# mLSTM row values spread over the partitions by DMA through DRAM, the experts' row numbers on GpSimd, and the launch's first loads in quarters

## The reference

```python
for layer in range(DEPTH):                       # DEPTH = 2
    h = rms_norm(x, norm1_w[layer])
    x = x + hybrid_mixer(h, w_in[layer], ...)    # z = h @ w_in; retention, dilated attention, mLSTM; gates; w_out
    h = rms_norm(x, norm2_w[layer])
    if layer % 2 == 0: x = x + swiglu(h, w_gate, w_up, w_down)
    else:              x = x + moe_swiglu(h, w_router, b_router, w_gate, w_up, w_down)

# in mlstm, per chunk; b is the running sum of the log forget gates, ib the input gate
D  = where(causal, b[:, None] - b[None, :] + ib[None, :], -inf)
m  = maximum(b + mm, max(D, -1));  Dw = exp(D - m[:, None])
s  = (q @ k.T) * Dw

# in moe_swiglu
logits = ht @ w_router + b_router
top_v, top_i = top_k(logits, 2);  probs = softmax(top_v)
for e in range(8):
    a = silu(ht @ w_gate[e]) * (ht @ w_up[e])
    out += gates[:, e:e+1] * (a @ w_down[e])
```

## Time and profile before

| | us |
|---|---|
| median of 3 runs | 1759.18 (1758.77 to 1760.2) |
| the profiled execution's own time | 1759.04 |
| its span | 1757.3 |
| PE busy | 1744.9 (99%) |
| DVE busy | 1388.0 (79%) |
| ACT busy | 1101.2 (63%) |
| POOL busy | 87.6 (5%) |

### The profile page before, as it was taken

The page is one execution under the profiler, slowest core; times in us unless marked ns, Lnnn a source line. Parts: engine busy times, 40 slices in busy tenths (PEclk is TensorE's granted clock), DMA queues, the critical chain, the costliest instruction groups (busy, mean ns, idle before and its releaser), DMA issues.

```text
span 1757.3 us, 22823 instructions
## 1 busy us (share of the span) xinstructions
PE 1744.9 (99%) x8418; PEld 1453.8 (83%) x8418; DVE 1388.0 (79%) x1179; ACT 1101.2 (63%) x976; POOL 87.6 (5%) x72
## 2 busy tenths in 40 slices
PE   9999999999999999999999999999999999999998
PEld 8888888888888888897888888888888888888887
DVE  7966587555688665879888889889888888898898
ACT  4445564434443566537777777777777777777775
POOL 1020000000000300001000000000000000000100
PEclk9999999999999999989999999999999999999999
DMA  8553365554445523557999999999999999999995
GB/s 318 192 192 120 120 240 216 192 191 133 179 168 176 183 72 121 214 216 264 400 348 413 381 351 407 373 365 396 347 399 385 348 413 372 358 403 373 369 413 197
DMA packets 218986, 497.11 MB, mean 283 GB/s; under 512 B 8080, under 2 KB 12432, under 8 KB 218768
## 3 DMA queue, kind: packets, MB, share of 16 engines
q1 hardware_dynamic: 215808, 483.70, 74.5%
q0 software_dynamic: 3120, 12.60, 1.8%
HBM read 490.49 MB, written 7.87 MB: 284 GB/s over the span
## 4 chain that ended last, share of the span: by engine, by line
PE 95%; DVE 2%; ACT 1%; DMA 1%; issue 0%; SPq 0%; DVEq 0%; ACTq 0%
PE ps L663 30%; PE ps L664 29%; PE ps L665 29%; PE ps L672 4%; PE ps L668 3%; DVE sb_wlo L395 1%; DMA sb_ringa<-in_w_in_dram 1%; ACT sb_w L1332 0%; DVE sb_wlo L366 0%; ACT sb_whi L359 0%; ACT sb_ahi L1389 0%; DVE sb_z L1706 0%; ACT L1332 0%; DVE sb_wlo L1657 0%; ACT sb_z L1382 0%
## 5 line engine op out<-in xcount | busy, mean ns | idle before, releaser
L395 DVE TENSOR_TENSOR sb_wlo<-sb_z,sb_whi 128x2048 fp32r<-128x2048 f32 x334 | 756.0, 2289 | 99.6 <-ACT sb_whi L389 99.0
L389 ACT ACTIVATE sb_whi<-sb_z 128x2048 fp32r<-128x2048 f32 x333 | 634.1, 1925 | 175.4 <-PE ps L665 171.2
L663 PE MATMUL ps<-sb_whi,sb_hhi 128*128 128x512 f32 (+1 forms) x1752 | 686.8, 392 | 3.5 <-DVE sb_wlo L395 2.5
L664 PE MATMUL ps<-sb_whi,sb_hlo 128*128 128x512 f32 (+1 forms) x1752 | 677.9, 387 | 0.0
L665 PE MATMUL ps<-sb_wlo,sb_hhi 128*128 128x512 f32 (+1 forms) x1752 | 677.5, 387 | 0.0
L663 PEld LDWEIGHTS ps<-sb_whi,sb_hhi 128*128 128x128 f32 x1752 | 329.7, 188 | 72.5 <-issue 4.5
L665 PEld LDWEIGHTS ps<-sb_wlo,sb_hhi 128*128 128x128 f32 x1752 | 329.6, 188 | 68.7
L664 PEld LDWEIGHTS ps<-sb_whi,sb_hlo 128*128 128x128 f32 x1752 | 330.0, 188 | 64.2
L366 DVE TENSOR_TENSOR sb_wlo<-sb_z,sb_whi 128x2048 fp32r<-128x2048 f32 (+1 forms) x74 | 158.5, 2146 | 82.1 <-ACT sb_whi L359 81.8
L359 ACT ACTIVATE sb_whi<-sb_z 128x2048 fp32r<-128x2048 f32 (+1 forms) x75 | 135.2, 1807 | 138.3 <-PE ps L665 138.2
L663 PE MATMUL ps<-sb_whi,sb_ahi 128*128 128x512 f32 x560 | 220.1, 393 | 1.1 <-DVE sb_alo L1614 1.1
(11 more groups left out here) (270 smaller groups left out, 986.5 us busy)
## 6 DMA issues: line engine op xcount, KB each, us to landing
sb_z<-in_moe_w_gate_dram SPq DMA_DIRECT2D x112, 1024.0 KB, 7.1
sb_z<-in_moe_w_up_dram SPq DMA_DIRECT2D x112, 1024.0 KB, 7.7
sb_z<-in_moe_w_down_dram SPq DMA_DIRECT2D x112, 1024.0 KB, 6.8
sb_ringa<-in_w_in_dram SPq DMA_DIRECT2D x43, 1024.0 KB, 4.8
sb_z<-in_w_in_dram SPq DMA_DIRECT2D x24, 1024.0 KB, 5.4
sb_z<-in_ffn_w_up_dram SPq DMA_DIRECT2D x10, 1024.0 KB, 5.0
sb_z<-in_ffn_w_gate_dram SPq DMA_DIRECT2D x10, 1024.0 KB, 4.9
sb_z<-in_ffn_w_down_dram SPq DMA_DIRECT2D x10, 1024.0 KB, 4.9
```

The costliest lines, as they stand in the source:

```text
L389: nc.scalar.activation(e_lane(s)[0], ringb[:, s % RING_B, :], ACT.Copy).then_inc(hi_done, 1)
L395: nc.vector.tensor_tensor(lo, ringb[:, s % RING_B, :], hi.bitcast(F32), ALU.subtract).then_inc(split, 1)
L663: nc.tensor.matmul(out, lh, rh, start=start, stop=False)
L664: nc.tensor.matmul(out, ll, rh, start=False, stop=False)
```

## The change

Three things. The mLSTM row values go to DRAM and come back to all partitions by DMAs of Pool, and the DVE adds the mask in place. The two batches `slots()` and `slot_ids()` leave the DVE; Pool computes the same numbers with other instructions (sums over eight experts are made by halving). The launch's first loads are cut in quarters, and the squares of x stand later on the DVE. The constants' load of the launch leaves out `sel` (512 of 4352 columns).

```diff
@@ -442,11 +444,13 @@
-            sp.dma_start(x[:, :, 0:C], xin[:, :, 0:C]).then_inc(x_in, 16)
+            sp.dma_start(x[:, :, 0:C // 2], xin[:, :, 0:C // 2]).then_inc(x_in, 16)
             sp.dma_start(const[:, 0:P], a["const"][:, 0:P]).then_inc(ident_in, 16)
             sp.dma_start(small[:, :], a["small"]).then_inc(small_in, 16)
-            first = part(a["w_in"][0], 0, KH // 2, IN_QK, C)
-            sp.dma_start(raw_slot(0, "A", 0)[:, 0:SLOT // 2].rearrange("p (k n) -> p k n", n=C), first).then_inc(raw_first, 16)
+            for k, landed in enumerate((raw_first, raw_second)):
+                sp.dma_start(raw_slot(0, "A", 0)[:, k * C:(k + 1) * C],
+                             a["w_in"][0][k * P:(k + 1) * P, IN_QK:IN_QK + C]).then_inc(landed, 16)
+            sp.dma_start(x[:, :, C // 2:C], xin[:, :, C // 2:C]).then_inc(x_more, 16)
@@ -462,7 +466,7 @@
                 if layer == 0:
-                    sp.dma_start(const[:, P:], a["const"][:, P:]).then_inc(consts_in, 16)
+                    sp.dma_start(const[:, P:CONST["sel"][0]], a["const"][:, P:CONST["sel"][0]]).then_inc(consts_in, 16)
@@ -566,6 +570,17 @@
+            def spread_rows(layer):
+                pool.wait_ge(rows_ok, layer + 1)
+                pool.dma_start(ml_rows, rows[:, 1, :]).then_inc(ml_stored, 16)
+                pool.wait_ge(ml_stored, 16 * (layer + 1))
+                pool.wait_ge(rpv_mm, layer + 1)
+                every = ml_rows.rearrange("(a b) s -> a b s", a=2).unsqueeze(0).to_broadcast([P, 2, 2, S])
+                for a_ in range(2):
+                    pool.dma_start(blkm[:, a_, :, 0:S], every[:, a_]).then_inc(spread_in, 16)
+                    pool.dma_start(blkm[:, a_, :, S:BLK], every[:, a_, :, P:S]).then_inc(spread_in, 16)
@@ -599,6 +614,7 @@
                 inverse_root(rrs, rss, RDV, root_ok)
+                spread_rows(layer)
                 inverse_root(mrs, mss, MDV, root_ok)
@@ -611,6 +627,68 @@
+            links = [0]
+            def link(ins):
+                links[0] += 1
+                ins.then_inc(pool_chain, 1)
+                pool.wait_ge(pool_chain, links[0])
+            rowx, item_ = lg, rtmp
+            both = stat(268, 32).rearrange("p (c t n) -> p c t n", c=2, t=TT)
+            pos = root[:, 0:16].rearrange("p (t n) -> p t n", t=TT)
+            part = root[:, 16:48].rearrange("p (c t n) -> p c t n", c=2, t=TT)
+            late, early = root[:, 48:50], root[:, 50:52]
+            term = root[:, 52:60].rearrange("p (a c t) -> p a c t", a=2, c=2)
+            per_token = lambda v: v.unsqueeze(1).to_broadcast([P, TT, NE])
+            per_choice = lambda v: v.unsqueeze(1).to_broadcast([P, 2, TT, NE])
+            def chosen(out, src):
+                link(pool.tensor_tensor(part, both, per_choice(src), ALU.mult))
+                link(pool.tensor_tensor(part[:, :, :, 0:4], part[:, :, :, 0:4], part[:, :, :, 4:8], ALU.add))
+                link(pool.tensor_tensor(part[:, :, :, 0:2], part[:, :, :, 0:2], part[:, :, :, 2:4], ALU.add))
+                link(pool.tensor_tensor(out.unsqueeze(3), part[:, :, :, 0:1], part[:, :, :, 1:2], ALU.add))
+            def low_then_high(out, first, second):
+                pool.tensor_tensor(term[:, 0, 0, :], first, early, ALU.mult)
+                pool.tensor_tensor(term[:, 0, 1, :], first, late, ALU.mult)
+                pool.tensor_tensor(term[:, 1, 0, :], second, late, ALU.mult)
+                link(pool.tensor_tensor(term[:, 1, 1, :], second, early, ALU.mult))
+                link(pool.tensor_tensor(out, term[:, 0], term[:, 1], ALU.add))
+            pool.wait_ge(route_ok, 1)
+            link(pool.tensor_scalar(selx, rank, float(NE - 1), None, ALU.add))
+            link(pool.tensor_tensor(selx, selx, iota[:, 0:NE], ALU.subtract))
+            link(pool.tensor_scalar(pos, posx, float(CAP) - 0.5, None, ALU.is_gt))
+            link(pool.tensor_tensor(item_, pos, per_token(selx), ALU.mult))
...
+            chosen(slotg, rowx)
+            chosen(slott, item_)
+            link(pool.tensor_tensor(early, slotg[:, 0, :], slotg[:, 1, :], ALU.subtract))
+            link(pool.tensor_scalar(late, early, 0.0, None, ALU.is_gt))
+            link(pool.tensor_scalar(early, late, -1.0, 1.0, ALU.mult, ALU.add))
+            low_then_high(slotx, slotg[:, 0, :], slotg[:, 1, :])
+            low_then_high(slotg, v12[:, :, 3], v12[:, :, 2])
+            pool.tensor_copy(idx[:, 0:2 * TT], slotx.rearrange("p c t -> p (c t)"))
+            pool.tensor_copy(idx[:, 6:6 + 2 * TT], slott.rearrange("p c t -> p (c t)")).then_inc(slots_ok, 1)
+            link(pool.tensor_scalar(rest[:, 0:1], eidf[:, 14:15], float(CAP), None, ALU.mult))
+            link(pool.tensor_tensor(tokf, slotx[:, 1, :], rest[:, 0:1].to_broadcast([P, TT]), ALU.subtract))
+            pool.wait_ge(gather_mm, 2)
+            for t in range(TT):
+                m = pool.tensor_scalar(pick[:, t, :], iota, tokf[:, t:t + 1], None, ALU.is_equal)
+            m.then_inc(late_pick, 1)
+            link(pool.tensor_scalar(rest, tokf, -0.5, None, ALU.is_gt))
+            link(pool.tensor_scalar(rest, rest, -1.0, 1.0, ALU.mult, ALU.add))
+            pool.tensor_tensor(rest, rest, slotg[:, 1, :], ALU.mult).then_inc(rest_ok, 1)
             pool.wait_ge(slots_ok, 1)
@@ -711,7 +788,7 @@
             pe.wait_ge(half_ok, 1)
-            for _ in range(20):
+            for _ in range(15):
...
             pe.wait_ge(ident_in, 16)
@@ -720,8 +797,10 @@
-                    turn_tokens(x, 0, ht_turned, (0, 1))
-                    warm(7)
+                    turn_tokens(x, 0, ht_turned, (0,))
+                    warm(6)
+                    pe.wait_ge(x_more, 16)
+                    turn_tokens(x, 0, ht_turned, (1,))
@@ -874,16 +953,8 @@
                     pe.wait_ge(dp_sb, layer * NG + g + 1)
                     weighted(6, lambda h: blkz[:, h // 2, h % 2, :], Z_DV + g * GH * DH, DH).then_inc(dpv_mm, 1)
-                def ml_spread():
-                    for h in range(MH):
-                        m = mm(ps[:, 4 + h // 2, h % 2 * S:(h % 2 + 1) * S], con("sel")[0:MH, h * P:(h + 1) * P],
-                               rows[:, 1, :])
-                    m.then_inc(msel_mm, 1)
...
-                    pe.wait_ge(mdw_in, L)
@@ -924,7 +995,7 @@
-                    (Q_G + 3, 0): (lambda: da_turn_p(2),), (Q_G + 3, 1): (lambda: da_out(2), ml_spread),
+                    (Q_G + 3, 0): (lambda: da_turn_p(2),), (Q_G + 3, 1): (lambda: da_out(2),),
                     (Q_G + 4, 0): (ml_scores,), (Q_G + 4, 1): (ml_out,),
@@ -1158,7 +1229,7 @@
-                    pe.wait_ge(pick_ok, 2)
+                    pe.wait_ge(late_pick, 1)
                     for t in range(TT):
@@ -1258,8 +1329,8 @@
-                    act.wait_ge(raw_first, 16)
-                    for k in range(KH // 2):
+                    for k, landed in enumerate((raw_first, raw_second)):
+                        act.wait_ge(landed, 16)
                         nc.scalar.activation(first[:, k * C:(k + 1) * C], raw[:, k * C:(k + 1) * C],
                                              ACT.Copy).then_inc(hi_first, 1)
                     turned_hi(0, ht_turned, 0, norm1, (1,))
@@ -1639,7 +1710,6 @@
-                    squares(0)
...
                     turned_lo(0, norm1, (0,))
@@ -1656,16 +1726,21 @@
+                turned_lo(3 * layer, norm1, (2, 3))
+                lo_a(2)
+                if layer == 0:
+                    dve.wait_ge(x_more, 16)
+                    squares(0)
...
                     total()
-                turned_lo(3 * layer, norm1, (2, 3))
-                lo_a(2)
+                    lo_a(3)
                 dve.wait_ge(rstd_ok, 2 * layer + 1)
...
                 m.then_inc(diag_ok, 1)
-                lo_a(3)
+                if layer > 0:
+                    lo_a(3)
@@ -1841,13 +1916,9 @@
                 lo_a(2 + 2 * (Q_G + 4))
                 da_keep(2)
-                dve.wait_ge(msel_mm, L)
-                sp_ = ps[:, 4:6, :].rearrange("p a (b s) -> p a b s", b=2)
+                dve.wait_ge(spread_in, 64 * L)
                 for a_ in range(2):
-                    V.tensor_tensor(blkm[:, a_, :, 0:S], sp_[:, a_], mlmask[:, 0:S].unsqueeze(1).to_broadcast([P, 2, S]),
-                                    ALU.add)
-                    m = V.tensor_tensor(blkm[:, a_, :, S:BLK], sp_[:, a_, :, P:S],
-                                        mlmask[:, S:BLK].unsqueeze(1).to_broadcast([P, 2, P]), ALU.add)
+                    m = V.tensor_tensor(blkm[:, a_], blkm[:, a_], mlmask.unsqueeze(1).to_broadcast([P, 2, BLK]), ALU.add)
                 m.then_inc(mdw_in, 1)
                 lo_a(3 + 2 * (Q_G + 4))
@@ -2066,9 +2136,6 @@
-                V.tensor_tensor(m1, m1, v12[:, :, 3:4].to_broadcast([P, TT, NE]), ALU.mult)
-                link(V.tensor_tensor(m2, m2, v12[:, :, 2:3].to_broadcast([P, TT, NE]), ALU.mult))
-                link(V.tensor_tensor(gatex[:, :, 0:NE], m1, m2, ALU.add))
@@ -2099,49 +2166,6 @@
```

(48 more changed lines are left out.)

19 lines of the change are left out of this document (removed).

## The result

The changed kernel takes 1747.34 us (median of 4, 1747.08 to 1749.65) against 1759.29 (4 runs of the kernel before on the same chip): ratio 0.9929 with a 95% interval of 0.9916 to 0.9941, so 11.95 us faster by the medians (the interval of the ratio is 10.4 to 14.8 us). One effect that the prediction has no term for, PE's clock, makes most of the difference. The profiled execution of the changed kernel took 1749.65 (span 1747.9), 2.3 above the other three, so between the two profiled executions the gain is 9.4.

The account below looks back on a forecast made before the run. PE, busy 1744.9 of 1757.3 us, was taken as the bound, so only work or waits taken off it count. -3.84 - 3.61 - 0.2 = -7.65 from 1759.04 gave 1751.4 us, range 1749.2 to 1755.0.

Parts of the forecast that it names:

- Part 1: mLSTM part, both layers: spreading rows by DMA takes the selector matmuls off PE, -3.84 us, between -3.4 and -3.9.
- the failed step: mLSTM part: layer 1 has the same eight selector-matmul records as layer 0, so PE loses 2 x 1.92 = 3.84 us.
- part 2: Experts' first item: slot numbers on Pool remove two PE waits (1.07 and 2.54 us), -3.6, between -2.4 and -4.2.
- Part 3: Launch: first loads in quarters and squares of x later, -0.2 us, between -1.0 and +1.0.
- A: Experts: Pool's chain ends after PE wants the picks, eating the whole gain from 844.9; 1790 at 2.29 a link; chance 0.06.
- B: Experts: Pool's reads hold the DVE so much that half the slot-number gain stays, 1753.2 us; chance 0.12.
- D: mLSTM part: matmuls taken off PE are half repaid by a late weight slot, 1 us a layer, 1753.4; chance 0.08.
- E: Experts: the slots' waits aren't the batches' doing, so only the mLSTM change counts, 1755.3 us; chance 0.07.
- C: Launch: Pool is not held and slot 1 lands no later, 1750.8 us; chance 0.12.
- the hold in the launch: Launch: the `lo_a(3)` subtraction on the DVE holds Pool's first root instruction, about 2 us long, until 26.9.
- `spread_in` in time: mLSTM part, layer 0: Pool's loads land by 171 at worst, the DVE asks at 214.8; cover 43 us, cost 0.
- The hold and the wait: Launch: Pool's held root delays the diagonals to 28.3, so PE waits 0.6 to 0.7 us for them.

Follow-up runs that it names:

- part 2 alone: The kernel before with only the slot-number batches moved from the DVE to Pool: 1755.36 us, ratio 0.9974, -3.7 us.

## Why the prediction was wrong in size, point by point

**Part 1, the failed step.** The step is "Layer 1 has the same eight records, so PE loses 2 x 1.92 = 3.84 us". The price of the matmuls was taken as their own time, and the half clock that comes with them was put at nothing, without a reason. The own time is about right (2.0 us a layer). What the sum lacks is 1.6 us each time that the clock falls, and 3.3 in the one long case: over the 12 stages with such matmuls (7 x 1.6 + 3.3) / 12 = 1.2 us a stage, 2.4 us an execution. I had followed the order in time to the product behind the matmuls for layer 0 only, where this one execution happened to keep the full clock, and took layer 1 for its copy; the rows from 688.38 on show the 0.63 us matmuls. The clock itself had been read before the forecast, as a mean of 0.97 from 600 to 780 and as 0.50 in the router's stretch, but no term and no rival was made of it.

The runs of all executions say the same by another way. The mean granted clock (given to 0.001) is 0.9961 over the 64 runs of before that stand beside the experiments, 2 x 0.0039 x 1757 = 14 us at half clock; it is 0.9977 over the 14 runs of the changed kernel, 8 us. These 6 us, at 0.39 to 0.47 us lost in each, are 2.3 to 2.8 us. (0.47 is from the spacing of the matmuls; 0.39 from the runs of before, of which 22 at 0.997 average 1758.0 and 17 at 0.995 average 1760.8.)

**The sum again.** Part 1 is -4.0 - 2.4 = -6.4, part 2 is -4.2, together -10.6 of the 11.95 measured by the medians. Part 3 adds nothing that can be told. The last 1.3 us is within the measurement's interval (10.4 to 14.8) and is left open.

**The rivals.** None of them held the clock: A, B, D and E take something away from the gain, and C adds only 0.6 in the launch. A, B and D are refuted: PE never waits for the picks, the whole 3.61 us of waits went, and nothing is repaid in the mLSTM part. E is refuted by part 2 alone (-3.7); its own time is 1755.2 by its one term, where 1755.3 stands. C has the lowest time (1750.8) and so lies nearest, 3.5 us off, but its reason is wrong: the hold in the launch is there.

**Part 1, the rest.** `spread_in` in time: right. The last issue is done at 148.0, and the loads land in the median 4.5 to 5.7 us behind their issue, so by about 154 where 171 was the worst.

**Part 2.** Right in mechanism; the size was 0.6 us short, since the waits were taken at their printed idle time (3.61) and were worth 4.20. Pool beside the DVE in the changed kernel, for the earlier trace rows:

```profile
787.93 0.22 POOL L650 TENSOR_TENSOR sb_root<-sb_root 128x16 f32<-128x16 f32 x1
788.23 2.32 POOL L651 TENSOR_TENSOR sb_root<-sb_root 128x8 f32<-128x8 f32 x1
790.63 2.13 POOL L652 TENSOR_TENSOR sb_st<-sb_root 128x4 f32<-128x4 f32 x1
792.83 2.18 POOL L649 TENSOR_TENSOR sb_root<-sb_st 128x32 f32<-128x32 f32 x1
...
807.80 1.22 POOL L687 TENSOR_SCALAR sb_z<-sb_const,sb_st 128x128 f32<-128x128 f32 x2
...
788.21 6.69 DVE L397 TENSOR_TENSOR sb_wlo<-sb_z,sb_whi 128x2048 fp32r<-128x2048 f32 x3
...
808.55 2.38 DVE L397 TENSOR_TENSOR sb_wlo<-sb_z,sb_whi 128x2048 fp32r<-128x2048 f32 x1 [0.30 <-ACT sb_whi L391]
```

Two kinds, 0.2 and 2.0 to 2.3 us, as forecast: three back-to-back subtractions let one instruction through each. The picks are ready at 809.0, not 818: 25 us after the chain's start instead of 29, and some 22 before PE wants them. The DVE is hardly held in return (2.38 for 2.29). The Trainium skill ("SBUF — State Buffer", § Who interferes with whom) has a VectorE instruction with two SBUF inputs contend with a GpSimd instruction that reads SBUF. The trace agrees: the long ones end within about 0.1 us of the end of such a subtraction, and up to 788.21, where none runs, each instruction takes 0.21 to 0.27 us.

**Part 3.** The hold and the wait came as forecast; a gain of 0.2 us is not shown, as executions differ by more. Changed kernel, the launch, for the earlier trace rows:

```profile
7.90 0.66 PE L749 MATMUL ps<-sb_const,sb_x 128*128 128x128 f32 x4 [1.52 <-DMA sb_x<-in_x_dram]
...
12.35 0.36 PE L740 MATMUL ps<-sb_hhi,sb_whi 128*128 128x256 f32 x1 [0.92 <-DVE sb_wlo L1722]
...
25.10 2.05 POOL L594 TENSOR_SCALAR sb_root<-sb_st 128x2 f32<-128x2 f32 x1 [24.07 <-DVE sb_st L1680]
...
28.01 0.72 DVE L1740 TENSOR_SCALAR sb_w<-sb_const,sb_st 128x128 f32<-128x128 f32 x2 [0.91 <-POOL sb_st L596]
```

PE starts its first product 1.6 us early (8.31 against 9.94), and gives it back to a wait of 0.92 for the next low part, to a slot that lands no earlier, and to the diagonals that wait for the held root. The root row starts at 28.87 in this trace and at 28.10 and 27.94 in those of the changed kernel run again; 28.3 was forecast. Over the nine traces with this launch it starts at 27.8 to 29.2, 28.3 in the mean; over the three with the old one at 27.7 to 28.5, 28.1 in the mean. PE's wait for the diagonals is 0.5 and 0.7; forecast 0.6.

**The range.** Its lower end summed the ends of the three parts, -9.1, and those ends held small shifts of single terms only: none of them had room for 1.6 us of clock a layer.

## What to carry to other kernels

- When work is taken off TensorE, read the granted clock and the spacing of the matmuls behind it, in every place where it stands and not in the first one only: its price is its own time plus what the clock does next. Here the own time was 4.0 us and the clock 2.4 in the mean.
- A matmul that uses a few rows to copy values over the partitions was dear twice here. If an engine or a queue with slack (here Pool's, 65 us ahead of need) can do the copy, the gain can be more than the matmul's time.
- Time at half clock differs between executions of one kernel (3.4, 6.9 and 10.2 us in the router's stretch of three traces of the changed kernel); one trace of each is not enough to compare a few us. Use the mean clock of all runs, and compare the length of the same stage over all traces.
- The two waits that went were worth 0.28 to 0.3 us more each than the idle time printed beside them. To price a wait, take the starts of the same matmul in both traces.

## What the runs showed of the hardware

The clock can fall without any idle time: PE is busy 4.00 of 4.00 us before and during the fall. At this place it fell with four rows in 8 of 12 stages and with 128 in none of 4. The Trainium skill ("TensorE: Matmul & The Clock Gate", § Why this matters for your kernels) puts drops in the middle of a kernel down to idle gaps between bursts; no gap stands here, so the measurement decides. Why four rows lead to it was not tried further.

The same eight records take 1.92 us to the next matmul with 4 rows (213.89 to 215.81) and 1.59 with 128 (213.67 to 215.26). A part of this comes back in the next product, and 0.3 us of stage length is left (2.0 against 1.7): fewer rows were not cheaper.

A second stretch at half clock is in the router's matmuls, which use all 128 rows, and all 14 traces have it: 3.4 to 10.2 us, in kernels with and without the 4-row matmuls. The kernel before, and the changed kernel as it ran beside the one with the squares moved:

```profile
772.00:776.00 4.00, 4.00 (x30) 4.00 (x29) 2.77 (x12) 2.88 (x6) 0.89 (x2) 0.73 0.65 241
776.00:780.00 4.00, 4.00 (x21) 4.00 (x21) 1.50 (x9) 1.33 (x2) 0.81 (x1) 0.50 0.18 73
780.00:784.00 4.00, 4.00 (x19) 4.00 (x20) 2.33 (x15) 0.09 (x1) 0.00 (x0) 0.50 0.47 189
```

```profile
772.00:776.00 4.00, 4.00 (x24) 4.00 (x23) 2.77 (x18) 0.21 (x1) 0.51 (x1) 0.57 0.66 264
776.00:780.00 4.00, 4.00 (x37) 3.91 (x37) 2.42 (x18) 0.00 (x0) 0.00 (x0) 1.00 0.01 4
```

It makes most of the spread between the profiled executions of the changed kernel. Those with 10.2 and with 3.4 us at half clock there took 1749.65 and 1745.78. From the turning of x behind the second mixer (758.61 in the first of them) to the experts' first product (786.61) it is 28.00 us in the one and 25.07 in the other, which is 2.9 of these 3.9 us; 0.9 is the launch.
